# An encoder layer with a bidirectional mLSTM: output gate as tanh, and three rounded passes in place of full-width products in three heads' chunk steps

## The reference, cut to what matters

```
a     = einsum('td,sd->ts', q, k) * exp(d - m_t)
num   = w_inter * (q @ C) + a @ v
den   = w_inter * (q @ n) + sum(a)
h     = num / max(|den|, exp(-m_t))
wk    = exp(g - m_new) * k
C_new = decay * C + wk^T @ v          # n_new the same with a column of ones
...
h = sigmoid(mo) * (h_fwd + h_bwd)
h = h * rsqrt(mean(h * h) + EPS) * norm_w
```

## Time and profile before

| | |
|---|---|
| median of 3 executions | 2499.71 us (2495.51 to 2500.24) |
| the profiled execution | 2500.26 us, of it a span of 2498.1 us |
| TensorE busy | 2449.7 us, 98% of the span |
| VectorE, ScalarE, GpSimd busy | 1211.4, 798.5, 1115.2 us |
| mean granted clock of TensorE | 0.996 |

### The profile page before, as it was taken

How to read it: one execution, slowest core, us unless ns; L and a number is a source line. 1 busy time by engine, 2 the same in 40 slices (tenths; PEclk the granted TensorE clock), 3 DMA queues, 4 the chain that set the end, 5 groups by cost and what they waited for, 6 DMA issues and landing times.

```text
span 2498.1 us, 33736 instructions
## 1 busy us (share of the span) xinstructions
PE 2449.7 (98%) x12862; PEld 2099.4 (84%) x12862; DVE 1211.4 (48%) x2158; ACT 798.5 (32%) x1633; POOL 1115.2 (45%) x1469
## 2 busy tenths in 40 slices
PE   7999999999999999999999999999999999999997
PEld 6888888888888888878888888888888888888886
DVE  6625566255753567375767625676311343300235
ACT  5213443234422443235432123433233222211222
POOL 3155520563116530365414495667566344332433
PEclk9999999999999999999999999999999999999998
DMA  3132111231122211224445433334334212222512
GB/s 132 55 110 81 60 39 42 96 97 42 35 82 79 81 37 32 93 76 138 133 142 165 132 127 133 112 128 159 138 132 142 96 67 93 67 79 79 181 60 76
DMA packets 127225, 240.38 MB, mean 96 GB/s; under 512 B 10568, under 2 KB 67496, under 8 KB 127064
## 3 DMA queue, kind: packets, MB, share of 16 engines
q1 hardware_dynamic: 85400, 206.09, 24.5%
q10 hardware_dynamic: 41664, 32.14, 4.5%
HBM read 187.50 MB, written 50.60 MB: 95 GB/s over the span
## 4 chain that ended last, share of the span: by engine, by line
PE 90%; DVE 6%; ACT 1%; DVEq 1%; issue 1%; POOL 1%; DMA 1%; ACTq 0%; SPq 0%; POOLq 0%
PE ps L2194 23%; PE ps L2196 23%; PE ps L2195 23%; PE ps L2242 3%; PE ps L2240 3%; PE ps L2241 3%; PE ps L2420 2%; PE ps L2330 2%; PE ps L2439 2%; PE ps L2345 2%; PE ps L2322 1%; PE ps L2453 1%; PE ps L2452 1%; PE ps L2312 1%; DVE small L1818 0%
## 5 line engine op out<-in xcount | busy, mean ns | idle before, releaser
L1008 POOL TENSOR_TENSOR unit_l<-unit_raw,unit_h 128x256 fp32r<-128x256 f32 x544 | 460.9, 882 | 476.1 <-ACT unit_h L1048 476.1
L2194 PE MATMUL ps<-ht_h,unit_h 128*128 128x512 f32 (+1 forms) x1408 | 509.7, 362 | 5.1 <-DVE gw L1854 4.4
L2196 PE MATMUL ps<-ht_h,unit_l 128*128 128x512 f32 (+1 forms) x1408 | 499.7, 355 | 0.0
L2195 PE MATMUL ps<-ht_l,unit_h 128*128 128x512 f32 (+1 forms) x1408 | 499.4, 355 | 0.0
L2194 PE MATMUL ps<-h_h,unit_h 128*128 128x512 f32 (+1 forms) x1056 | 378.1, 358 | 0.0
L2195 PE MATMUL ps<-h_l,unit_h 128*128 128x512 f32 (+1 forms) x1056 | 377.6, 358 | 0.0
L2196 PE MATMUL ps<-h_h,unit_l 128*128 128x512 f32 (+1 forms) x1056 | 377.2, 357 | 0.0
L878 POOL TENSOR_TENSOR unit_h<-unit_raw,colt 128x256 fp32r<-128x256 f32 x320 | 201.1, 659 | 353.9 <-DMA unit_raw<-w 353.5
L2194 PEld LDWEIGHTS ps<-ht_h,unit_h 128*128 128x128 f32 x1408 | 267.2, 190 | 42.8 <-issue 6.0
L2196 PEld LDWEIGHTS ps<-ht_h,unit_l 128*128 128x128 f32 x1408 | 266.7, 189 | 37.5
L2195 PEld LDWEIGHTS ps<-ht_l,unit_h 128*128 128x128 f32 x1408 | 267.2, 190 | 35.8 <-issue 0.2
(11 more groups left out here) (283 smaller groups left out, 4250.4 us busy)
## 6 DMA issues: line engine op xcount, KB each, us to landing
unit_raw<-w SPq DMA_DIRECT2D x229, 512.0 KB, 3.4
bw<-exponent_rows_scratch ACTq DMA_DIRECT2D x40, 256.0 KB, 3.7
gate_scratch<-g_st SPq DMA_DIRECT2D x28, 256.0 KB, 3.6
ym_scratch<-y_st ACTq DMA_DIRECT2D x40, 128.0 KB, 1.9
ya_scratch<-ya_st ACTq DMA_DIRECT2D x40, 128.0 KB, 2.5
zo_scratch<-o_st SPq DMA_DIRECT2D x36, 128.0 KB, 1.7
xs<-xt SPq DMA_DIRECT2D x2, 2048.0 KB, 15.0
gw<-gate_scratch SPq DMA_DIRECT2D x16, 256.0 KB, 3.0
```

What stands on the lines that cost most here:

```text
L1008: last = nc.gpsimd.tensor_tensor(unit_l[:, slot, k:k + 2], unit_raw[:, slot, k:k + 2], unit_h[:, slot, k:k + 2].bitcast(F32), ALU.subtract)
L2194: mm(out_ap, wh, hi(k + k_first), start=first and k == 0, stop=False)
L2195: mm(out_ap, wh, lo(k + k_first), start=False, stop=False)
L2196: ins = mm(out_ap, wl, hi(k + k_first), start=False, stop=last and k == kts - 1)
```

## The change

Output gate: ScalarE takes the hyperbolic tangent of half the gate once, in `gate_o`, when `evac_vo` has written a block and before it is stored; `gated` multiplies by one plus the loaded value. The exponential, the added one and the reciprocal go away. The factor two is taken out in `rstd` (`scale=0.25 / DH`) and by halving the norm's weights at the start. The tangent's tables are loaded at the start and before each attention stage, those of the logarithm in step 3 of each `mlstm`. In head 0 ScalarE stores six blocks of the gate in place of four.

In heads 0 to 2, values, weights and scaled keys are split in a high and a low part, and each full-width product with the values becomes three rounded passes of 258, 258 and 256 columns. The products with the state stay. The splits are new instructions: values in pairs of chunks, `round_values` and `values_high` on ScalarE and `values_low` on VectorE; weights, `weights_high` on ScalarE and `weights_low` on VectorE; keys, `keys_high` on ScalarE and `keys_low` on GpSimd, each direction with its own semaphore. `v_lo` lies where `aq_t` will be written, so groups 15 to 18 move by a step. The scores of the next step always go ahead of the first group. The load of the biases waits for the updates of the head, since `wk_h` lies there.

The core of the diff:

```diff
-A_STEPS = [[2], [3, 4], [5, 6], [7], [8, 9], [10, 11], [12, 13], [14, 15], [16, 17], [18]]
+A_STEPS = [[2], [3, 4], [5, 6], [7], [8, 9], [10, 11], [12, 13], [14], [15, 16], [17, 18]]
...
# TensorE, m_numden (heads 0 to 2)
-                    ins = mm(ps[:, 3 + d, 0:DH + 1], ex[i % 2][:, side(d, i)], v_tok[:, chunk_of(d, i)],
-                             start=True, stop=fresh(d, i))
+                        mm(ps[:, 3 + d, 0:DH + 2], ex_h[i % 2][:, d], v_hi[:, c], start=True, stop=False)
+                        mm(ps[:, 3 + d, 0:DH + 2], ex_l[:, i % 2, d, 0], v_hi[:, c], start=False, stop=False)
+                        ins = mm(ps[:, 3 + d, 0:DH], ex_h[i % 2][:, d], v_lo[:, low_place(c)], start=False,
+                                 stop=fresh(d, i))
...
# TensorE, m_update (heads 0 to 2)
-                pe.wait_ge(m_wk, lin(lambda k: 9 * k + i + 1, h))
+                pe.wait_ge(m_wk[d], 8 * h + updates_to(d, i))
-                    ins = mm(ps[:, 5 + dt, 0:DH + 1], wk[:, d, dt * P:(dt + 1) * P], v_tok[:, chunk_of(d, i)],
-                             start=True, stop=True)
+                    mm(ps[:, 5 + dt, 0:DH + 2], wk_h[:, d, half], v_hi[:, c], start=True, stop=False)
+                    mm(ps[:, 5 + dt, 0:DH + 2], wk_l[:, d, half], v_hi[:, c], start=False, stop=False)
+                    ins = mm(ps[:, 5 + dt, 0:DH], wk_h[:, d, half], v_lo[:, low_place(c)], start=False, stop=True)
...
# GpSimd, in step i
                     scale_queries(i + 1, h)
-                    if i + 1 < NB - 1:
-                        scale_keys(i + 1, h)
+                    if whole:
+                        for d in range(2):
+                            scale_keys(d, i + 1, h, m_wk)
+                    else:
+                        scale_keys(0, i + 1, h, m_ks)
                     if i + 2 < NB:
                         mask_rows(i + 2, h)
+                    if not whole:
+                        keys_low(0, i + 1, h)
+                        scale_keys(1, i + 1, h, m_ks)
+                        keys_low(1, i + 1, h)
...
                     if h < HEADS - 1 and i in A_TAKE:
                         take(lambda k, u=A_TAKE.index(i) + 2: a_unit(k, u), h)
...
+            def keys_low(d, i, h):
+                if not updates(d, i):
+                    return
+                pool.wait_ge(m_kh[d], 8 * h + updates_to(d, i))
+                nc.gpsimd.tensor_tensor(wk_l[:, d], wk[:, d], wk_h[:, d].bitcast(F32), ALU.subtract
+                                        ).then_inc(m_wk[d], 1)
...
# ScalarE, heads 0 to 2, step i (whole and new)
+                for i in range(NB if dense else 0):
+                    if 1 <= i < NB - 1:
+                        exponents(i + 1, h)
+                    if i + 1 < NB // 2:
+                        round_values(i + 1, h)
+                    if i == 3:
+                        nc.scalar.preload_act_table_set("natural_log_exp_and_others")
+                    if i > 5:
+                        finish_y(i - 1, h)
+                    if i + 1 < NB // 2:
+                        keep_scores(i + 1, h)
+                    keys_high(0, i + 1, h)
+                    if i + 1 < NB:
+                        weights_high(i + 1, h)
+                    evac_a(a_steps(h)[i][0], h)
+                    if i + 2 < NB:
+                        load_rows(i + 2, h)
+                    if i + 1 < NB // 2:
+                        values_high(i + 1, h)
+                    keys_high(1, i + 1, h)
+                    for g in a_steps(h)[i][1:]:
+                        evac_a(g, h)
+                    if i >= 5:
+                        rstd(i, h)
+                    if 3 <= i < NB - 2:
+                        load_o(i + 2, h)
...
+            def weights_high(i, h):
+                act.wait_ge(m_am, NB * h + i + 1)
+                nc.scalar.activation(ex_h[i % 2][:], bw[:, i % 2, :, 0], ACT.Identity).then_inc(m_eh, 1)
+            def keys_high(d, i, h):
+                if updates(d, i):
+                    act.wait_ge(m_ks[d], 8 * h + updates_to(d, i))
+                    nc.scalar.activation(wk_h[:, d], wk[:, d], ACT.Identity).then_inc(m_kh[d], 1)
...
# ScalarE, the gate, in head 0's start and in attend
+            def gate_o(blk, h):
+                act.wait_ge(ev_dve, GROUPS[("M", h, 12 + blk)][3])
+                nc.scalar.activation(o_st[:, blk % 2], o_st[:, blk % 2], ACT.Tanh, scale=0.5).then_inc(m_ot, 1)
...
# VectorE
-                    V.tensor_tensor(h_acc[:, ch[d]], h_acc[:, ch[d]], o[:, d], ALU.mult)
+                    V.scalar_tensor_tensor(h_acc[:, ch[d]], o[:, d], 1.0, h_acc[:, ch[d]], ALU.add, ALU.mult)
...
+            def weights_low(i, h):
+                dve.wait_ge(m_eh, NB * h + i + 1)
+                V.tensor_tensor(ex_l[:, i % 2, :, 0], bw[:, i % 2, :, 0], ex_h[i % 2][:].bitcast(F32), ALU.subtract
+                                ).then_inc(m_a, 1)
...
                     if i + 1 < NB:
                         weights(i + 1, h)
+                    if dense and i + 1 < NB // 2:
+                        values_low(i + 1, h)
+                    if dense and i + 1 < NB:
+                        weights_low(i + 1, h)
                     if i >= 5:
                         gated(i, h)
-                    if 5 <= i + 1 < NB:
-                        gate_ahead(i + 1, h)
                     state(1, i, h)
```

## The result

| | before | after |
|---|---|---|
| median | 2499.91 us (2495.51 to 2500.24, 4 executions) | 2538.98 us (2537.39 to 2540.99, 4 executions) |
| profiled execution, span | 2500.26, 2498.1 us | 2539.82, 2538.0 us |

The changed kernel is slower: the ratio is 1.016, 95% interval 1.0147 to 1.0173. The forecast was 2541.5.

What follows compares the result with a forecast made beforehand. TensorE, busy 98% of the span, was taken to bound the kernel, with no slack in heads 0 to 2. Net waits 45.6, clock 5.1 and last head -8.9 gave +41.8 us, so 2541.5; range 2503 to 2580, own range 2520 to 2560.

Steps and rivals of the forecast that it cites:

- The passes: Heads 0 to 2, TensorE: three rounded passes save 0.075 us for each of 52 products, 3.9 us a head.
- The loop: Heads 0 to 2, GpSimd and ScalarE: 15.1 us between issues of rows; forward low keys ready 5.15 us after issue.
- rival (b): Heads 0 to 2: only landing of rows binds; waits into steps 4 and 8 and transposes remain; 2503 us, chance 0.10.
- The waits: Heads 0 to 2: TensorE waits for low keys, weights and transposes, into steps 2 to 8, 19.1 us a head.
- the prediction's own sign: Heads 0-2: TensorE waits 10 to 15 us each for GpSimd's low keys, most before steps 2, 4, 5 and 8.
- What took the weights' place: Value products in heads 0 to 2 wait for the weights' low part: 1.2 us into step 2, 0.65 into step 5.
- The clock: Step 8 of heads 0 to 2: TensorE's clock falls once a head, 1.7 us lost each, 5.1 in all.
- The last head: Last head keeps full-width products but loses the reciprocals, 3.34 us each: 8.9 us come back, bounds 5 and 10.
- Attention stages, moved groups, scores: Tanh in attention costs nothing; moving groups 15 to 18 changes no total; scores ahead is free on TensorE, doesn't help.
- The total: Whole kernel: 45.6 + 5.1 - 8.9 = +41.8 us, giving 2541.5 us; own range 2520 to 2560, chance 0.67.
- Rival (a): Heads 0 to 2: the clock's price falls at all eight waits a head, 1.7 us each; 2577 us, chance 0.12.
- Rival (c): Heads 0 to 2: low keys are in time, so only gains stay, -20.6 us; 2479 us, chance 0.11.

Runs made afterwards that it cites:

- e6: e4 with, on ScalarE, the scaling of an output by its norm ahead of the backward keys' rounding and the second group's evacuation: 2482.88 us.
- e2: The changed kernel with ScalarE's rounding of the forward keys moved behind weights, values, first evacuation and issue of the rows: 2517.71 us.
- e4: e2 with GpSimd's mask of rows moved behind both directions' scaled keys and low parts: 2488.87 us.
- e8: The changed kernel with GpSimd's mask behind both directions' low keys in step 7 alone: 2515.93 us.
- e7: The changed kernel with scaled keys left whole, update products full-width and the values' low part left out of the updates: 2494.45 us.
- e11: e6 with scores behind the backward update in steps 1 and 2, where ScalarE evacuates and issues rows before copying scores: 2484.86 us.
- e3: The changed kernel with the edits of e1 and e2 together: 2506.84 us.
- e5: The kernel before with the output gate as tanh and nothing else of the change: 2491.21 us.
- e9: e6 with GpSimd's mask ahead of the low keys again in step 7 alone: 2500.66 us.
- e1: The changed kernel with GpSimd's subtraction for the forward low keys ahead of the masking of rows, heads 0 to 2: 2527.05 us.
- e10: e6 with scores behind the backward update, their copy behind the rows' issue, and weights' rounding behind the first evacuation in every step: 2502.78 us.

## Why the prediction was right

The place, the sign and the size hold: 2541.5 against 2538.98. Step by step, in us a head where nothing else is said:

- **The passes.** 0.075 saved for each product, 3.9; e6 shows 0.069 and 3.6, and 0.074 and 3.8 when the busy time of its one wait is taken off. The new matmuls start 0.12 apart, as said.
- **The loop.** 15.1 us from one issue of rows to the next was forecast; it is 14.4 (482.67 to 497.11) in the trace. The forward low keys are ready 4.79 us behind the issue (482.67 to 487.46), forecast 5.15. e2, which cuts the loop, leaves just the waits of rival (b): in head 1 the idle time ahead of steps 1, 2, 3, 5 and 6 goes from 6.7 us to 0.55, that of steps 4 and 8 stays (6.9 and 7.6). So ScalarE's place behind the keys is shown to be the cause of the rest, but for one thing: 1.7 us of it, the waits for the values in steps 1 and 2, may have gone with the rounding of the values, which the same edit moved. e4, which cuts both turns, leaves 0.30 us of the waits for low keys.
- **The waits.** 19.1 was forecast. In the stage of head 1 TensorE is idle for 159.80 - 146.05 = 13.75, and with the busy time of eleven waits, 2.2 to 3.0 us, it is 16.0 to 16.7. By step, idle time alone: into step 1 0.73 (forecast none), step 2 2.35 (4.15), step 3 0.3 (1.45), step 4 1.6 (2.3), step 5 1.8 (2.8), step 6 1.5 (2.7), step 8 5.3 (5.7). The three longest come in the order forecast. By kind, the waits for the low keys are 7.8 us (forecast 13.0; the prediction's own sign, 10 to 15 us a head on GpSimd's low part, was missed), those of the transposes 2.8 (4.25), those of the value products 3.0 (1.85). Two things make the keys' part smaller. The loop is shorter: set on the first value product (443.9 in the forecast, 460.41 here), the issue of step 1 is where it was forecast (482.67), and those of steps 4, 5 and 6 are 1.5, 2.1 and 2.4 us early (the last at 550.22). And TensorE comes later: it is ready for the update of step 2 at 486.15, forecast 484.96, since it had waited for values and its own work took longer than the prices said.
- **What took the weights' place.** The value products were forecast to wait for the weights' low part; they wait for the values' high part, 7.0 us in nine waits (all three heads), because `values_high` stands last on ScalarE, behind the rows. A value product in step 5 waits another 0.54 us in each head, which the trace puts down to nobody. The forecast looked at the values only at the start of a head, where indeed there is no wait.
- **The clock.** One fall a head was right. Its price, 1.7 from the last head of before, was low: 2.5 to 3.3, by e8. In the last head of before the lower clock lasted 3.4 us, here 6.8 to 10.2. The terms of head 1, 16.0 to 16.7 for the waits, 2.5 or so for the clock and -3.8 for the passes, make 14.7 to 15.4 against +15.3 by the stages; forecast were 19.1 + 1.7 - 3.9 = 16.9. The mis-sized term is the waits, 2.4 to 3.1 too high; the clock, about 1 too low, goes against it.
- **The last head.** -8.9 was forecast, it is -6.8. From the evacuation of the group before the first value product to that of the twelfth group it is now 93.0 us (1076.45 to 1169.43), forecast 90.9. The waits left are 0.5 for the queries and 0.7 for the transposes, where 1 was forecast; the rest, 1.8 us, lies in TensorE's own work, 91.7 where the sum of prices had 89.9. Of the -6.8, 4.2 is idle time (5.66 to 1.49) and 2.6 busy time (120.53 to 117.90), the fall of the clock in it.
- **Attention stages, moved groups, scores.** Forecast at nothing, they are: +0.2, +0.1, +0.2; e7; e11, where the scores ahead are worth 0.7 a head, so that they give nothing was nearly right.
- **The total.** That 2541.5 lies only 2.5 us from the measured time is partly luck. The three heads were forecast at +50.7 and came at +45.9, 4.8 too high; the last head was 2.1 too low, and the stretches outside the stages add 0.8 that nobody forecast. The prediction's own range, 2520 to 2560, does not quite come out of its terms either: 13 us of net waits and no fall give 2530, 19 us and three falls 2563.

Rival (a), a fall at every wait, is refuted by the trace and by e8: in the three heads waits of up to 1.7 us left the clock at 1.00. It had been given the rule of the Trainium skill ("TensorE: Matmul & The Clock Gate", the section on HAM oscillation). The page tells of short bursts with longer waits between them, each of which brings the lower clock. That case stood here only in step 8, a wait of 4 us and then 1.2 to 1.7 us of work up to the next wait, and there the clock fell; in the other steps the work between two waits lasted longer than either (1.8 us between waits of 0.99 and 1.36 at the least), and it didn't. So the rule did not speak for this rival. Rival (b) has its waits in e2, and not its time: 2503 was worked out without the three falls of the clock, the extra wait of 0.55 and the last head's 2.1 us, together some 11 of the 14.7 us that are missing. Rival (c), faster, needed the keys in time; e6 shows what that is worth when the order allows it: 2482.9, where its sum gave 2479.

Left open: what it takes for the clock to fall. In the chunk stages a wait of 3.9 us or more brought it every time (15 of them), and none of up to 1.8 us did. Between them the length of the wait alone does not decide. In the stages the 2.14 us of e2 left the clock at 1.00, and the 2.7 us of the earlier trace rows, behind three shorter ones, did not. In the attention of the last head each of the 13 kernels has a wait of 1.94 to 2.14 us for VectorE's `gw`, with no other wait in the 40 us ahead of it: the clock fell behind it in ten kernels, before and after among them, and not in e3 (2.08), e5 (2.10) and e6 (1.94). In before:

```profile
1329.26 0.47 PE L2194 MATMUL ps<-ht_h,unit_h 128*128 128x512 f32 x1 [2.14 <-DVE gw L1854]
...
1330.00:1334.00 4.00, 4.00 (x12) 3.13 (x12) 3.92 (x7) 2.01 (x5) 2.74 (x1) 0.60 0.59 201
```

and in e6:

```profile
1313.59 0.47 PE L2324 MATMUL ps<-ht_h,unit_h 128*128 128x512 f32 x1 [1.94 <-DVE gw L1984]
...
1312.00:1316.00 4.00, 2.41 (x11) 2.00 (x12) 4.00 (x8) 4.00 (x9) 0.62 (x1) 1.00 1.08 389
```

## What to carry to other kernels

When an operand is split, the new subtraction has a place in a queue, and it is its neighbours that price it: ask for each added instruction what the one ahead of it waits for. Here a mask that waits for a transfer and a rounding that waits for another engine closed a loop of 14.4 us around steps of 12 to 15; in the order of e6 TensorE waits 0.3 us once a head for the same instructions, and 39 us lost become 17 won. Put what waits for a DMA last in a step, put the issue of a DMA ahead of what waits for another engine, and look for one long wait first: it is paid a second time in the clock.

## What the runs showed of the hardware

- The granted clock of TensorE went to 0.50 (1.2 GHz) behind each wait of 3.9 us or more in the chunk stages (3.92 to 4.31 in e9, 4.04 to 4.20 in after, 4.00 to 4.36 in e2, 4.52 to 4.85 in e3, 5.05 to 5.53 in e1), never there behind waits of up to 1.8 us, though there were 9.5 us of these in one stage (e8). Behind waits of about 2 us it fell or it didn't (2.14 in e2, clock 1.00; 2.14 in the last head's attention of before, 0.60 in the four microseconds behind it).
- The fall can come in the wait or behind it: in e9 the first matmuls behind the wait of head 1 still start 0.12 us apart and only 0.6 us later 0.19 and 0.21, while in head 0 they are at 0.21 and 0.22 at once. Its price goes with the time at the lower level: 1.3 and 1.5 us for 3.4 us of it and 2.6 for 6.8 (e9), 2.5 to 3.3 for 6.8 to 10.2 (after, by e8).
- A wait costs TensorE 0.20 to 0.27 us beside its idle time (e4, e10 and e8 against e6), so busy time of two kernels is not compared as if it were work.
- A full-width product of 257 columns costs 0.435 us, three rounded passes in its place 0.36 by the starts and 0.361 to 0.366 by the whole stage of e6: the switch between the two kinds costs next to nothing.
